# A Strassen product in the gate/up layers of a two-model forward pass

## The reference, cut to what matters

```python
def _rmsnorm(x, g):
    xf = x.astype(jnp.float32)
    y = xf * lax.rsqrt(jnp.mean(xf * xf, axis=-1, keepdims=True) + EPS)
    return (y * g.astype(jnp.float32)).astype(x.dtype)

def _swiglu(h, wg, wu, wd):
    return (jax.nn.silu(h @ wg) * (h @ wu)) @ wd

# first model, twice
h = rmsnorm(x, g_pre_ffn[l])
gate, up = jnp.split(h @ w_ffn_in[l], 2, axis=-1)
f = (jax.nn.silu(gate) * up) @ w_ffn_out[l]
# second model, twice in each of two layers
h = _rmsnorm(x, ffn_pre_norm[l])
x = x + 0.5 * _swiglu(h, ffn_pre_w_gate[l], ffn_pre_w_up[l], ffn_pre_w_down[l])
```

## Time and profile before

| | us |
|---|---|
| median of 3 runs | 3278.37 |
| lowest, highest | 3277.93, 3278.74 |
| span of the profiled execution | 3276.4 |
| PE busy in the span | 3233.9 |
| DVE, ACT, POOL busy | 1244.3, 1160.8, 1606.0 |

### The profile page before, as it was taken

One profiled execution on the slowest core, in us unless ns is written; L12 is line 12 of the kernel. 1 busy time (PEld: TensorE's weight loads), 2 busy tenths in 40 slices (PEclk: granted clock), 3 DMA queues, 4 the chain that ended last, 5 costly groups with the idle time before them and its releaser, 6 DMA issues.

```text
span 3276.4 us, 43120 instructions
## 1 busy us (share of the span) xinstructions
PE 3233.9 (99%) x15554; PEld 2637.2 (80%) x15554; DVE 1244.3 (38%) x2059; ACT 1160.8 (35%) x1838; POOL 1606.0 (49%) x839
## 2 busy tenths in 40 slices
PE   9999999999999999999999999999999999999999
PEld 7678888886788887888888778888888887788887
DVE  4743124567531245511444242124311443331134
ACT  4653222556532224422333432222322333332222
POOL 4546444665464446644465245444544453354444
PEclk9999999999999999999999999999999999999999
DMA  4112222221122222322222112222222222122222
GB/s 157 50 55 100 96 96 96 84 100 52 52 103 96 96 96 84 126 96 96 96 90 85 57 65 103 96 96 96 99 96 96 97 97 71 65 90 96 96 97 70
DMA packets 82397, 293.82 MB, mean 90 GB/s; under 512 B 9035, under 2 KB 11467, under 8 KB 82028
## 3 DMA queue, kind: packets, MB, share of 16 engines
q1 hardware_dynamic: 80944, 286.06, 24.9%
q10 hardware_dynamic: 1340, 6.23, 0.5%
HBM read 290.15 MB, written 2.10 MB: 89 GB/s over the span
## 4 chain that ended last, share of the span: by engine, by line
PE 93%; DVE 2%; POOL 2%; issue 2%; ACT 1%; DMA 0%; SPq 0%; POOLq 0%; DVEq 0%; ACTq 0%
PE bank L2115 29%; PE bank L2116 28%; PE bank L2117 28%; PE bank L2644 1%; PE bank L2624 1%; POOL w_lo L610 1%; PE bank L2731 1%; POOL diag L745 1%; PE bank L2486 0%; PE bank L2766 0%; PE bank L2446 0%; PE bank L2464 0%; PE bank L2128 0%; ACT y L1098 0%; PE bank L2917 0%
## 5 line engine op out<-in xcount | busy, mean ns | idle before, releaser
L610 POOL TENSOR_TENSOR w_lo<-w_raw,w_hi 128x1024 fp32r<-128x1024 f32 (+1 forms) x538 | 1299.6, 2420 | 1415.3 <-ACT w_hi L839 1371.3
L2115 PE MATMUL bank<-mvh,w_hi 128*128 128x512 f32 (+1 forms) x4454 | 1711.1, 384 | 10.6 <-DVE mvl L1446 2.9
L2117 PE MATMUL bank<-mvh,w_lo 128*128 128x512 f32 (+1 forms) x4454 | 1688.8, 379 | 0.0
L2116 PE MATMUL bank<-mvl,w_hi 128*128 128x512 f32 (+1 forms) x4454 | 1688.1, 379 | 0.0
L839 ACT ACTIVATE w_hi<-w_raw 128x1024 fp32r<-128x1024 f32 x537 | 568.2, 1060 | 1727.6 <-PE bank L2117 1711.8
L2115 PEld LDWEIGHTS bank<-mvh,w_hi 128*128 128x128 f32 x4454 | 837.9, 188 | 200.8 <-issue 35.1
L2117 PEld LDWEIGHTS bank<-mvh,w_lo 128*128 128x128 f32 x4454 | 837.7, 188 | 159.0
L2116 PEld LDWEIGHTS bank<-mvl,w_hi 128*128 128x128 f32 x4454 | 838.5, 188 | 149.8 <-issue 0.2
L1509 DVE TENSOR_TENSOR scr<-bank,rstd_b 128x512 f32<-128x512 f32 x264 | 181.2, 690 | 994.5 <-PE bank L2117 990.6
L1526 DVE TENSOR_TENSOR mvl<-big,mvh 128x512 fp32r<-128x512 f32 x132 | 270.0, 2056 | 346.7 <-ACT mvh L997 346.7
L745 POOL TENSOR_TENSOR diag<-diag,scr 128x512 f32<-128x512 f32 (+1 forms) x144 | 160.4, 1114 | 19.0 <-ACT scr L857 3.0
(11 more groups left out here) (226 smaller groups left out, 1669.4 us busy)
## 6 DMA issues: line engine op xcount, KB each, us to landing
w_raw<-in_weights SPq DMA_DIRECT2D x537, 512.0 KB, 3.2
x<-in_x SPq DMA_DIRECT2D x8, 256.0 KB, 7.9
out_y<-y SPq DMA_DIRECT2D x8, 256.0 KB, 2.2
tab<-in_dist ACTq DMA_DIRECT2D x2, 640.0 KB
tab<-in_gmlp ACTq DMA_DIRECT2D x2, 640.0 KB
tab<-in_ret_dil ACTq DMA_DIRECT2D x1, 1280.0 KB
y<-in_p ACTq DMA_DIRECT2D x2, 512.0 KB, 3.5
y<-in_rotary ACTq DMA_DIRECT2D x1, 1024.0 KB
```

The lines of the kernel that those rows point to most:

```text
L610: last = nc.gpsimd.tensor_tensor(w_lo[:, slot, at], w_raw[:, slot, at], w_hi[:, slot, at].bitcast(F32), ALU.subtract)
L2115: nc.tensor.matmul(bank[:, at], hi, mvh[:, k, at], start=first, stop=False, skip_group_check=again)
L2116: nc.tensor.matmul(bank[:, at], hi, mvl[:, k, at], start=False, stop=False, skip_group_check=again)
L2117: return nc.tensor.matmul(bank[:, at], lo, mvh[:, k, at], start=False, stop=last, skip_group_check=again)
```

## The change

The first 12 units (6 pairs) of each gate/up layer stay as they are. Each of the other 16 pairs becomes one product of 2x2 blocks: the rows of the left matrix are gate and up, its columns the two halves of the 1024 features; the right matrix is split by the same halves of the features and by two halves of the tokens (256 columns each). Seven block products take the place of eight. Each block product has 4 tiles with three matmuls of 256 columns each, 12 matmuls.

The left operands are A11, A12, A22 and four sums of blocks (`S1` to `S4`). VectorE makes the sums, ScalarE the high parts of all seven, and VectorE the low parts; GpSimd has no part in the 16 pairs. The right operands are the normalised activations and their combinations (`B11`, `B21`, `B22`, `T1` to `T4`); VectorE and ScalarE make them once a layer, in the course of the plain pairs. Since they are already normalised, the scaling by `rstd_b` falls away for these pairs. The results stand in two PSUM banks a pair (6 and 7, or 4 and 5). ScalarE copies three partial results out (`parted`, `fifth`), and VectorE joins them (L1810 `g`, L1816 `u`). The last block product of a pair, A22 by T4 (`fourth`), is issued in the next pair, after its second product. VectorE's `hidden` (L1783) multiplies silu(gate) by up.

SyncE's loads are placed by hand around the pairs. The loads of tables before two layers of the second model move from ahead of the gate/up layer to the start of the down layer (ScalarE's queue). The down layer's first four units are split by ScalarE and GpSimd as the slots of the last pair come free (`down_high`).

In the diff `st_hi`, `st_lo`, `st_sum`, `st_prod`, `st_copy` and `st_u` count high parts, low parts, sums, block products, copies and joined ups. `form_hi` and `form_lo` count the parts of the right operands.

```diff
+PLAIN, PAIRS_ST = 12, 16
+BLOCK = UNIT // 2
+A11, A12, S1, S3, S2, S4, A22 = range(7)
+B11, T1, T2, B21, B22, T3, T4 = range(7)
...
+        w_lo, w_sum = sb_shared("w_lo", [P, RING, UNIT], F32, F32R)
...
+        class Pairs:
...
+                self.high = {B11: wide(scr_r[:, 8:10, :]), T1: tabs[0], T2: tabs[1]}
+                self.high.update(zip((B21, B22, T3, T4), late))
...
+                def body(t, p):
+                    sp.wait_ge(st_lo, t * 14 + st.lo0 + 7 * (p - 1) + 2)
+                    load_pair(t, p)
...
+                def period(t, p):
+                    q = p + 1
+                    product_done(t, p, 1)
+                    if p == 0:
+                        act.wait_ge(hidden_ready, st.f0)
+                    else:
+                        ge(act, bank_free, t * 2 + st.g0 + p - 1)
+                    nc.scalar.activation(parted[:, p % 2, 0:S // 2], st.chain_bank(p)[:, 0:S // 2],
+                                         ACT.Copy).then_inc(st_copy, 1)
+                    sum_high(t, p, S3)
+                    if q < PAIRS_ST:
+                        raw_high(t, q, A11, 0, 0)
+                    product_done(t, p, 2)
+                    if p >= 2:
+                        act.wait_ge(st_u, t * 2 + st.u_0 + p - 1)
+                    nc.scalar.activation(fifth[:, p % 2, :], st.side_bank(p)[:, S // 2:S], ACT.Copy).then_inc(st_copy, 1)
+                    if q < PAIRS_ST:
+                        sum_high(t, q, S1)
+                    if p:
+                        product_done(t, p, 3)
+                    raw_high(t, p, A22, 1, 1, 1 if q < PAIRS_ST else 3)
+                    product_done(t, p, 4)
+                    nc.scalar.activation(parted[:, p % 2, S // 2:S], st.chain_bank(p)[:, 0:S // 2],
+                                         ACT.Copy).then_inc(st_copy, 1)
+                    if q < PAIRS_ST:
+                        sum_high(t, q, S2)
+                        product_done(t, p, 5)
+                        raw_high(t, q, A12, 0, 1)
+                    else:
+                        down_high(name, 0)
+                    act.wait_ge(bank_free, t * 2 + st.g0 + p + 1)
+                    g = g1[:, p % 2, :]
+                    nc.scalar.activation(g, g, ACT.Silu).then_inc(silu_done, 1)
+                    if q < PAIRS_ST:
+                        sum_high(t, q, S4)
...
+                act.wait_ge(unit_done, L.u0 + PLAIN)
+                for form in (B21, B22, T3, T4):
+                    form_high(form)
+                period(0, 0)
+                period(0, 1)
...
-                    cast(0, f)
-                after_unit(lin[in_name], 0, 2 * FT - 1)
+                cast(0, 0)
+                for i in range(1, 4):
+                    down_high(in_name, i)
+                    if i < 3:
+                        cast(0, i)
+                    if i == 2:
...
+                def form_low(form):
+
+                    order = (B11, T1, T2, B21, B22, T3, T4)
+                    dve.wait_ge(form_hi, st.form0 + order.index(form) + 1)
+                    nc.vector.tensor_tensor(st.low[form], st.full[form], st.high[form].bitcast(F32),
+                                            ALU.subtract).then_inc(form_lo, 1)
+                def low(form, src, more, n=1):
+                    nc.vector.tensor_tensor(st.lo(form, n), src, st.hi(form, n).bitcast(F32),
+                                            ALU.subtract).then_inc(st_lo, more)
...
+                def second_sum(t, q):
+                    sum_ready(t, q, 1)
+                    summed(t, q, S2, st.sum(S1), st.raw(q, 0, 0))
...
+                def hidden(t, p):
+
+                    product_done(t, p + 1, 3)
+                    dve.wait_ge(silu_done, t * 2 + st.f0 + p + 1)
+                    dve.wait_ge(st_u, t * 2 + st.u_0 + p + 1)
+                    dst = big[:, bass.ds(t * 2 + PLAIN // 2 + p, 1), :].rearrange("p a b -> p (a b)")
+                    nc.vector.scalar_tensor_tensor(out=dst, in0=st.chain_bank(p)[:, :], scalar=-1.0,
+                                                   in1=g1[:, p % 2, :], op0=ALU.mult,
+                                                   op1=ALU.mult).then_inc(hidden_ready, 1)
+
+                def period(t, p):
+                    q = p + 1
+                    more = q < PAIRS_ST
+                    if more:
+                        high_ready(t, q, 2)
+                        low(A11, st.raw(q, 0, 0), 1)
+                        product_done(t, p, 2)
+                        first_sum(t, q)
+                    if p:
+                        hidden(t, p - 1)
+                    high_ready(t, q, 4)
+                    low(A22, st.raw(p, 1, 1), 1 if more else 2)
+                    if more:
+                        product_done(t, p, 4)
+                        second_sum(t, q)
+                        sum_ready(t, q, 2)
+                        low(S1, st.sum(S1, 2), 2, 2)
+                        high_ready(t, q, 6)
+                        low(A12, st.raw(q, 0, 1), 1)
+                    else:
+                        low(S3, st.sum(S3), 2)
+                    product_done(t, p, 6)
+                    dve.wait_ge(st_copy, t * 6 + st.copy0 + 3 * p + 3)
+                    nc.vector.tensor_tensor(g1[:, p % 2, :], st.side_bank(p)[:, :], parted[:, p % 2, :],
+                                            ALU.add).then_inc(bank_free, 1)
+                    if more:
+                        fourth_sum(t, q)
+                    product_done(t, p, 7)
+                    chained = st.chain_bank(p)
+                    nc.vector.tensor_tensor(chained[:, S // 2:S], chained[:, 0:S // 2], fifth[:, p % 2, :],
+                                            ALU.add).then_inc(st_u, 1)
+                    if more:
+                        third_sum(t, q)
+                        high_ready(t, q, 7)
+                        low(S2, st.sum(S2, 2), 2, 2)
+
...
+                    unit(11)
+                    for form in (B21, B22, T3, T4):
+                        form_low(form)
+                    period(0, 0)
+                    period(0, 1)
+                    pair_loop(dve, 2, PAIRS_ST - 2, period)
+                    period(0, PAIRS_ST - 2)
+                    period(0, PAIRS_ST - 1)
+
...
+                def product(t, p, bank, weight, n_hi, n_lo, form, begin, more=1):
+
+                    if p == 0:
+                        order = (B11, T1, T2, B21, B22, T3, T4)
+                        pe.wait_ge(form_hi, st.form0 + order.index(form) + 1)
+                        pe.wait_ge(form_lo, st.form0 + order.index(form) + 1)
+                    pe.wait_ge(st_hi, t * 14 + st.hi0 + 7 * p + n_hi)
+                    high, low = st.high[form], st.low[form]
+                    for k in range(4):
+                        w = st.hi(weight)[:, k * P:(k + 1) * P]
+                        nc.tensor.matmul(bank, w, high[:, k, :], start=(begin and k == 0), stop=False,
+                                         skip_group_check=True)
+                        nc.tensor.matmul(bank, w, low[:, k, :], start=False, stop=False, skip_group_check=True)
+                    pe.wait_ge(st_lo, t * 14 + st.lo0 + 7 * p + n_lo)
+                    for k in range(4):
+                        w = st.lo(weight)[:, k * P:(k + 1) * P]
+                        last = nc.tensor.matmul(bank, w, high[:, k, :], start=False, stop=(k == 3),
+                                                skip_group_check=True)
...
+                def fourth(t, p, more=1):
+
+                    pe.wait_ge(st_u, t * 2 + st.u_0 + p + 1)
+                    product(t, p + 1 if p else 0, st.chain_bank(p)[:, 0:S // 2], A22, 4 if p else 11, 2 if p else 9, T4,
+                            False, more)
+
+                def copied(t, p, n):
+                    pe.wait_ge(st_copy, t * 6 + st.copy0 + 3 * p + n)
+
+                def period(t, p):
+                    chained, left, right = (st.chain_bank(p)[:, 0:S // 2], st.side_bank(p)[:, 0:S // 2],
+                                            st.side_bank(p)[:, S // 2:S])
+                    if p == 1:
+                        pe.wait_ge(bank_free, st.g0)
+                    elif p:
+                        pe.wait_ge(hidden_ready, t * 2 + st.f0 + p - 1)
+                        pe.wait_ge(bank_free, t * 2 + st.g0 + p - 1)
+                    product(t, p, chained, A11, 2, 1, B11, True)
+                    product(t, p, right, S1, 3, 4, T1, True, 1 if p else 2)
+                    if p:
+                        fourth(t, p - 1)
+                    copied(t, p, 1)
+                    product(t, p, chained, S2, 5, 7, T2, False)
+                    copied(t, p, 2)
+                    product(t, p, left, A12, 6, 5, B21, False)
+                    product(t, p, right, S4, 7, 7, B22, False)
+                    copied(t, p, 3)
+                    product(t, p, chained, S3, 8, 11, T3, False)
+
+                for p in range(2):
+                    period(0, p)
```

(32 more changed lines are left out.)

251 lines of the change are left out of this document (207 added, 44 removed).

## The result

| | before | changed |
|---|---|---|
| median (runs) | 3278.27 us (6) | 3289.41 us (6) |
| lowest to highest | 3277.93 to 3278.85 | 3288.45 to 3290.22 |
| span of the profiled execution, granted clock | 3276.4, 0.999 | 3286.6, 0.991 |

The ratio is 1.0033 with a 95% interval of 1.0022 to 1.0045: the changed kernel is 0.33% slower, 11.1 us. Forecast was +14.3 us (3292.7).

A forecast was written before the change was run, and what follows sets the result against it. TensorE, busy 99% of the span, was taken to bound the kernel. Terms -76.8 + 29.4 + 4.7 + 43.2 + 13.8 = +14.3 us, added to 3278.4, gave 3292.7 us; range 3246 to 3318, a tenth left out at each end.

The forecast's parts named there:

- 96 pairs: Middle of the gate/up layers: 84 matmuls at 0.120 us replace 48 at 0.2267, 10.08 us for 10.88 a pair, -76.8 us.
- entry: Start of the 16 pairs: TensorE waits 1.85, 1.6 and 1.45 us for ScalarE and VectorE, 4.9 a layer, +29.4 us.
- last `u`: End of pair 16: matmul tail, the join `u` and two handoffs take 0.75 us a layer, +4.7 us in all.
- exit: Start of the down layer: GpSimd's splits delay VectorE's low parts and `hidden`; TensorE waits 7.2 us a layer, +43.2 us.
- half pace at the exit: After the long wait entering the down layer: TensorE loses full clock, 2.3 us a layer, +13.8 us.
- The pair is bound by TensorE: Inside a pair: VectorE's 8.4 us and ScalarE's 5.1 us fit in TensorE's 10.08, so no added cost, 0.
- reserve of 1 us: Inside a pair: the other engines' work and the loads fit beside TensorE's with 1 us to spare.
- Rival D: Pair loop: not bound by TensorE, through register operations, handoffs or late loads; 0.2 us a pair gives 3312 us; chance 13%.
- Taking turns: Entering the down layer: if VectorE's low parts and GpSimd's splits alternate, the end is the same within 0.6 us.
- Rival C: Entering the down layer: VectorE gets the port after GpSimd's unit 2; wait 2.5 us, no clock lost, 3251 us; chance 23%.
- Rival B: Entering the down layer: TensorE's clock holds through the wait, giving 3279 us, no change; chance 20%.

The follow-up runs named there:

- run with three operations more: Changed kernel with three more VectorE operations (a block sum made again) in each of the 96 pairs: 3400.66 us.
- run with one: Changed kernel with one more VectorE operation (a block sum made again) in each of the 96 pairs: 3291.78 us.
- `hidden` first: Changed kernel with VectorE making the last pair's `hidden` after the first of the down layer's four low parts, not after the fourth: 3236.23 us.
- GpSimd later: Changed kernel with GpSimd splitting down units 2 to 4 only after the four low parts are made, VectorE's order unchanged: 3245.59 us.
- both kernels with work in the wait: Changed kernel with extra, unused TensorE matmuls of 512 columns in the wait before bank 4: 3276.18 us with 27, 3287.61 us with 15.

## Why the prediction was right, point by point

| term | forecast us | read from the trace us | by itself |
|---|---|---|---|
| 96 pairs | -76.8 | -76.8 (10.08 each) | not isolated |
| entry | +29.4 | +27.5 | order changed: 13.4 of it back |
| last `u` | +4.7 | +4.1 | not tried |
| exit | +43.2 | +39.0 | with the clock: 53.2 |
| half pace at the exit | +13.8 | +13.9 | 13.2 |
| half pace at an entry | 0 | +1.4 | |
| sum | +14.3 | +9.1 | the span grew by 10.2 |

**Matmuls.** 0.120 and 10.08 us, as the earlier trace rows had it. No run isolates the saving; the two periods in the traces, 10.88 and 10.08 us, are its evidence.

**The pair is bound by TensorE.** Right, and so is the reserve of 1 us: 0.97 by the run with three operations more, and the pair unmoved at 10.08 us by the run with one. VectorE was 8.55 us for 8.4 forecast, ScalarE 5.73 for 5.1. Rival D falls.

**Entry.** The gaps are 1.55, 1.50 and 1.53 us for 1.85, 1.6 and 1.45: 4.58 a layer for 4.9. The first was 0.3 too large; the third came 0.1 longer. The releasers are the three that were named. In one layer (from 2396.5 us) the clock dipped as well, 1.4 us, which the forecast had not allowed for after waits this short. In the profiled executions of the other kernels with the same three waits it did so in three of six layers (`hidden` first) and in two of six (GpSimd later, and both kernels with work in the wait).

**Last `u`.** 0.68 us for 0.75.

**Exit.** 6.50 us for 7.2. The total was 0.7 us off, but two parts of it were further off and partly cancel, which is luck. I let GpSimd's queued splits go first, as in the earlier trace rows, and the three low parts follow the last of them by 2.0 us; the trace has the two engines in turn, and the last low part done 0.55 us after the last split, 1.45 less. For the same reason the splits, held up by the low parts between them, took 7.91 us for 7.17 and ended 8.9 us after `fourth` started, for 8.1. Taking turns was named, with the end put at within 0.6 us. That the splits hold the low parts up is shown by delaying GpSimd, that VectorE's order is a cause too by moving `hidden`. The wait needs both: without the one 1.1 us of the 6.3 are left, without the other nothing. Rival C falls: VectorE got the next turn after GpSimd's unit 2, as it supposed, but for one operation, and two more splits lay before the last low part.

**Clock.** 13.9 us, by six stretches that lost 2.7, 3.0, 1.9, 1.9, 1.6 and 3.0 us (rounded; with the pace put at 0.2267 us throughout they come to 14.1). The forecast of 2.3 each came from one cold start; that the mean is right is partly luck, as a single start could give neither it nor the scatter of a factor of two. Rival B falls: with matmuls in the wait the same kernel is 13.2 us faster. This agrees with "TensorE: Matmul & The Clock Gate", "HAM oscillation", of the Trainium skill, which the prediction named: the full clock was gone behind six of six waits of 6.3 us.

About 1.1 us of the growth of the span is assigned to nothing. The sum came within 3.2 us of the 11.1 measured because every large term was close, though entry and exit were 6.1 us too dear together, and the dip at an entry and the unassigned part took 2.5 of that back.

## What to carry to other kernels

When a faster inner loop is put between other loops, add up its two ends as carefully as its middle: here 96 pairs gave 76.8 us and twelve ends took 86, with the clock. Look at each end for an operation that the bottleneck engine waits for and that stands in a list behind work that nobody wants yet; moving it by one line was worth 53 us. Where several engines work off arrears, a better order shifts a wait before it removes one, so time each order, and count a wait of the matmul engine at its length plus what the clock takes behind it.
